# Full 128 by 128 tiles in the attentions of the second block

## The reference

```
proj = h @ w_in              # queries, keys, values, forget gates, branch gates
qa, ka = rms_norm(...)       # first attention: 8 heads of 64
log_f = log_sigmoid(fa + forget_bias);  c = cumsum(log_f)
# first attention, for head h, query i, key j <= i (16 learned tokens included)
s = qa.ka / 8 + c_i - c_j ;  p = softmax(s) ;  o_fox = p @ va
# second attention: 8 query heads of 64 over 2 key heads, a window of 128,
s = qb.kb / 8 + bias_by_distance ;  p = softmax(s with a sink) ;  o_swa = p @ vb
y = sigmoid(ga) * (o_fox @ w_branch_fox) + sigmoid(gb) * (o_swa @ w_branch_swa)
h = h + y @ w_out
```

## Time and profile before

| | |
|---|---|
| median of three runs | 2533.72 us |
| the profiled execution: time, span | 2534.61, 2532.8 us |
| TensorE busy | 2481.2 us, 98% |
| VectorE, ScalarE busy | 1899.5 us (75%), 1251.7 us (49%) |
| GpSimd busy | 125.7 us, 5% |
| DMA | 467.22 MB, 184 GB/s |

### The profile page before, as it was taken

One profiled execution on the slowest core, in us unless ns is written; L12 is line 12 of the kernel. 1 busy time (PEld: TensorE's weight loads), 2 busy tenths in 40 slices (PEclk: granted clock), 3 DMA queues, 4 the chain that ended last, 5 costly groups with the idle time before them and its releaser, 6 DMA issues.

```text
span 2532.8 us, 48392 instructions
## 1 busy us (share of the span) xinstructions
PE 2481.2 (98%) x17792; PEld 2279.1 (90%) x17792; DVE 1899.5 (75%) x3685; ACT 1251.7 (49%) x2079; POOL 125.7 (5%) x99
## 2 busy tenths in 40 slices
PE   9999999999999999999999999999999999999999
PEld 8999988999999889999989999998889998778999
DVE  6789997666666887889986666666877756667774
ACT  6754874444444434556864444444344445445443
POOL 0042000000000000061000000000000000000000
PEclk9999999999999999999999999999999999999999
DMA  7445677666655554445776666655545553534555
GB/s 241 142 153 177 194 203 237 210 207 208 215 194 188 185 188 167 167 160 190 199 236 214 208 211 207 211 185 188 189 152 175 171 187 124 110 126 136 181 179 163
DMA packets 192505, 467.22 MB, mean 184 GB/s; under 512 B 81747, under 2 KB 83795, under 8 KB 191457
## 3 DMA queue, kind: packets, MB, share of 16 engines
q1 hardware_dynamic: 118736, 419.99, 50.0%
q0 software_dynamic: 6992, 25.81, 3.7%
q10 hardware_dynamic: 66624, 19.40, 3.2%
HBM read 442.53 MB, written 22.61 MB: 184 GB/s over the span
## 4 chain that ended last, share of the span: by engine, by line
PE 48%; DVE 3%; DMA 1%; ACT 1%; issue 0%; DVEq 0%; ACTq 0%
PE acc L842 14%; PE work L522 9%; PE work L524 9%; PE work L523 9%; PE acc L522 1%; PE acc L523 1%; PE work L856 1%; PE acc L524 1%; DMA ring<-in_gate_in 1%; DVE ring_lo L516 1%; PE work L1071 1%; PE work L1043 0%; PE work L695 0%; DVE arena L2125 0%; PE work L697 0%
## 5 line engine op out<-in xcount | busy, mean ns | idle before, releaser
L516 DVE TENSOR_TENSOR ring_lo<-ring,ring_hi 128x1024 fp32r<-128x1024 f32 x758 | 920.2, 1217 | 431.3 <-ACT ring_hi L510 429.6
L510 ACT ACTIVATE ring_hi<-ring 128x1024 fp32r<-128x1024 f32 (+1 forms) x798 | 832.6, 1051 | 460.5 <-PE acc L842 369.9
L522 PE MATMUL work<-normed_hi,ring_hi 128*128 128x256 f32 (+1 forms) x2512 | 715.3, 285 | 21.3 <-DVE ring_lo L516 13.9
L523 PE MATMUL work<-normed_lo,ring_hi 128*128 128x256 f32 (+1 forms) x2512 | 709.4, 282 | 0.0
L524 PE MATMUL work<-normed_hi,ring_lo 128*128 128x256 f32 (+1 forms) x2512 | 707.1, 281 | 0.0
L842 PE MATMUL acc<-ring_hi,weighed 128*128 128x512 f32 x2048 | 588.3, 396 | 4.8 <-DVE weighed L1947 4.8
L522 PEld LDWEIGHTS work<-normed_hi,ring_hi 128*128 128x128 f32 x2512 | 473.5, 189 | 35.7 <-DVE ring_lo L516 13.7
L523 PEld LDWEIGHTS work<-normed_lo,ring_hi 128*128 128x128 f32 x2512 | 474.7, 189 | 7.9
L524 PEld LDWEIGHTS work<-normed_hi,ring_lo 128*128 128x128 f32 x2512 | 473.4, 188 | 0.0
L842 PEld LDWEIGHTS acc<-ring_hi,weighed 128*128 128x128 f32 x2048 | 373.7, 188 | 83.8 <-DVE weighed L1947 5.2
L522 PE MATMUL work<-arena_parts,ring_hi 128*128 128x256 f32 (+1 forms) x1184 | 337.5, 285 | 1.8 <-ACT arena L1151 1.1
(11 more groups left out here) (289 smaller groups left out, 2505.3 us busy)
## 6 DMA issues: line engine op xcount, KB each, us to landing
ring<-in_u SPq DMA_DIRECT2D x256, 512.0 KB, 3.3
ring<-in_v SPq DMA_DIRECT2D x256, 512.0 KB, 3.3
ring<-in_ffn_in SPq DMA_DIRECT2D x88, 512.0 KB, 3.3
ring<-in_query SPq DMA_DIRECT2D x32, 512.0 KB, 3.3
ficients_of_later_chunks<-gate_b ACTq DMA_DIRECT2D x32, 512.0 KB, 4.6
arena<-ficients_of_later_chunks POOLq DMA_DIRECT2D x32, 512.0 KB, 4.1
ring<-in_ffn_out SPq DMA_DIRECT2D x32, 512.0 KB, 3.9
ring<-in_even_in SPq DMA_DIRECT2D x27, 512.0 KB, 4.2
```

Source lines behind the costliest of these rows:

```text
L510: act.activation(ring_hi[:, n % RING, 0:width], ring[:, n % RING, 0:width], ACT.Copy).then_inc(hi_ready, 1)
L516: eng.tensor_tensor(ring_lo[:, n % RING, 0:width], ring[:, n % RING, 0:width], ring_hi[:, n % RING, 0:width].bitcast(F32), ALU.subtract).t ...
L522: pe.matmul(out, w_hi, hi, start=start, stop=False, **more)
L523: pe.matmul(out, w_hi, lo, start=False, stop=False, **more)
```

## The change

The transposes, value products and key bias are made of full 128 by 128 tiles. Rows of `scores2` grow from 276 to 384 columns, and the buffer moves onto rows of `forget` that are done with. The last block of values is cleared once, so that its rows behind the 16 are zero, and each of the two value heads of the second attention is stored twice side by side. The value product writes all 128 partitions, of which the half of the head is read. The high and low part of the cumulated gates stand in partitions 0 to 7 and 32 to 39 of one zeroed tile, and the signs likewise, so that the bias is one product over 128 partitions. The signs (`neg_head`) are read as 128 partitions in place of 8. GpSimd has two more clearings at the start of its part and, at the end of it, clears the columns behind each row of `scores2`; TensorE waits for these (`pads_ready`) ahead of its first two turns.

```diff
         val2 = view("mix", [6, 3, P])
+        scores2 = arena[:, forget_at + TA:forget_at + TA + 4 * 3 * P].rearrange("p (b t) -> p b t", b=4)
...
+            pool.memset(val2[:, :, 2, :], 0.0).then_inc(memset_done, 1)
+            pool.memset(forget_two[:, :].bitcast(F32), 0.0).then_inc(memset_done, 1)
...
-                             (neg_head[0:FOXH, :, :], a["neg_head"]),
+                             (neg_head[:, :, :], a["neg_head"]),
...
                     pool.dma_start(bias2[:, t, :, lo:lo + width], src).then_inc(bias_in, 16)
+            pool.wait_ge(*freed(W0["mix"] + MIX_ITEMS.index(("turnf", 0))))
+            pool.wait_ge(forget_lo, 1)
+            for t in range(NT):
+                n = META + P * (t + 1)
+                pool.memset(scores2[:, t::NT, n:P * (t + 2)], 0.0).then_inc(pads_ready, 1)
...
-                            for x in range(2):
-                                mm = pe.matmul(work[:, w % 4, 0:keys], neg_parts[0:FOXH, h, :], forget_two[0:FOXH, x, 0:keys], start=False, stop=(x == 1))
+                            mm = pe.matmul(work[:, w % 4, 0:keys], neg_parts[:, h, :], forget_two[:, 0:keys], start=False, stop=True)
...
                         pe.wait_ge(probs_ready, n_before + u + 1)
+                        if u < NT:
+                            pe.wait_ge(pads_ready, NT)
                         for b in range(t + 2):
-                            lo, hi = b * P, min((b + 1) * P, keys)
-                            mm = pe.transpose(work[0:hi - lo, w % 4, b * P:(b + 1) * P], scores2[:, u % 4, lo:hi], ident)
+                            mm = pe.transpose(work[:, w % 4, b * P:(b + 1) * P], scores2[:, u % 4, b * P:(b + 1) * P], ident)
...
-                            v = val2[0:rows, h // 2, b, (h % 2) * HD2:(h % 2 + 1) * HD2] if fox else \
-                                val2[0:rows, 4, b, (h // 4) * HD2:(h // 4 + 1) * HD2]
-                            mm = pe.matmul(work[half, w % 4, t * P:S], v, prob2[0:rows, u % 2, b, t:NT, :].rearrange("p t q -> p (t q)"),
+                            v = val2[:, h // 2 if fox else 4 + h // 4, b, :]
+                            mm = pe.matmul(work[:, w % 4, t * P:S], v, prob2[:, u % 2, b, t:NT, :].rearrange("p t q -> p (t q)"),
...
                     elif kind == "swaval":
                         act.wait_ge(*done(w))
-                        act.activation(val2[:, 4, 0:2, :], work[:, w % 4, 0:S].rearrange("p (t d) -> p t d", t=2), ACT.Copy)
-                        act.activation(val2[0:META, 4, 2, :], work[0:META, w % 4, S:S + P], ACT.Copy).then_inc(bank_free[w % 4], 1)
+                        for g in range(2):
...
+                            act.activation(twice(val2[:, 4 + g, 0:2, :]), main.unsqueeze(2).to_broadcast([P, 2, 2, HD2]), ACT.Copy)
+                            ins = act.activation(val2[0:META, 4 + g, 2, :].rearrange("p (x d) -> p x d", x=2), meta.unsqueeze(1).to_broadcast([META, 2, HD2]), ACT.Copy)
...
-                    act.activation(prob2[:, h % 2, 0:t + 1, t, :], work[:, w % 4, 0:(t + 1) * P].rearrange("p (b q) -> p b q", q=P), ACT.Copy)
-                    act.activation(prob2[0:META, h % 2, t + 1, t, :], work[0:META, w % 4, (t + 1) * P:(t + 2) * P], ACT.Copy).then_inc(bank_free[w % 4], 1)
+                    if t:
+                        empty(w, prob2[:, h % 2, :, t, :], work[:, w % 4, 0:3 * P].rearrange("p (b q) -> p b q", q=P))
+                    else:
...
```

More of the change, by code:

```diff
@@ L55 @@
 NB = 32
+HALF_ROW = 32
 EVEN_ITEMS = [
@@ L399, in build @@
         qk2raw = view("mix", [BEHIND, TA])
-        scores2_at = used["mix"]
         qk2sq = view("mix", [BEHIND, TA])
-        scores2 = arena[:, scores2_at:scores2_at + 4 * (TA + 4)].rearrange("p (b t) -> p b t", b=4)
         qk2ms = view("mix", [BEHIND, TA])
         bias2 = view("mix", [NT, FOXH, TA])
-        val2 = view("mix", [5, 3, P])
+        val2 = view("mix", [6, 3, P])
         prob2 = view("mix", [2, 3, 2, P])
@@ L421, in build @@
         w_forget = view("mix", [K, FOXH])
+        forget_two = view("mix", [TA], arena_parts)
         mix_y = view("after", [2, S])
@@ L1067, in attend @@
                         for b in range(NT + 1):
[L1068 to L1071 removed]
+                            t = max(b - 1, 0)
+                            v = val2[:, h // 2 if fox else 4 + h // 4, b, :]
+                            mm = pe.matmul(work[:, w % 4, t * P:S], v, prob2[:, u % 2, b, t:NT, :].rearrange("p t q -> p (t q)"),
                                            start=(b == 0), stop=(b == NT), skip_group_check=True)
@@ L1484, in mix @@
                     elif kind == "lastval":
+                        if j == 0:
+                            act.wait_ge(memset_done, 9)
                         empty(w, val2[0:META, 2 * j:2 * j + 2, 2, :], work[0:META, w % 4, 0:S].rearrange("p (h d) -> p h d", h=2))
@@ L1487, in mix @@
                         act.wait_ge(*done(w))
-                        act.activation(val2[:, 4, 0:2, :], work[:, w % 4, 0:S].rearrange("p (t d) -> p t d", t=2), ACT.Copy)
-                        act.activation(val2[0:META, 4, 2, :], work[0:META, w % 4, S:S + P], ACT.Copy).then_inc(bank_free[w % 4], 1)
+                        for g in range(2):
+                            twice = lambda v: v.rearrange("p t (x d) -> p t x d", x=2)
+                            cols2 = slice(g * HD2, (g + 1) * HD2)
+                            main = work[:, w % 4, 0:S].rearrange("p (t d) -> p t d", t=2)[:, :, cols2]
+                            act.activation(twice(val2[:, 4 + g, 0:2, :]), main.unsqueeze(2).to_broadcast([P, 2, 2, HD2]), ACT.Copy)
+                            meta = work[0:META, w % 4, S + g * HD2:S + (g + 1) * HD2]
+                            ins = act.activation(val2[0:META, 4 + g, 2, :].rearrange("p (x d) -> p x d", x=2), meta.unsqueeze(1).to_broadcast([META, 2, HD2]), ACT.Copy)
+                        ins.then_inc(bank_free[w % 4], 1)
                     elif kind == "turnf":
                         act.wait_ge(forget_ready, 1)
-                        act.activation(forget_two[0:FOXH, 0, :], forget[0:FOXH, 0, :], ACT.Copy).then_inc(forget_hi, 1)
+                        act.activation(forget_two[0:FOXH, :], forget[0:FOXH, 0, :], ACT.Copy).then_inc(forget_hi, 1)
                         empty(w, forget_col, work[:, w % 4, 0:NT * FOXH].rearrange("p (t h) -> p t h", t=NT))
@@ L1522, in turn_copy @@
                         act.wait_ge(*done(w0 + ATT_ITEMS.index(("mix", h - 2))))
-                    act.wait_ge(*done(w))
-                    act.activation(prob2[:, h % 2, 0:t + 1, t, :], work[:, w % 4, 0:(t + 1) * P].rearrange("p (b q) -> p b q", q=P), ACT.Copy)
-                    act.activation(prob2[0:META, h % 2, t + 1, t, :], work[0:META, w % 4, (t + 1) * P:(t + 2) * P], ACT.Copy).then_inc(bank_free[w % 4], 1)
+                    if t:
+                        empty(w, prob2[:, h % 2, :, t, :], work[:, w % 4, 0:3 * P].rearrange("p (b q) -> p b q", q=P))
+                    else:
+                        act.wait_ge(*done(w))
+                        act.activation(prob2[:, h % 2, 0, t, :], work[:, w % 4, 0:P], ACT.Copy)
+                        act.activation(prob2[0:META, h % 2, 1, t, :], work[0:META, w % 4, P:2 * P], ACT.Copy).then_inc(bank_free[w % 4], 1)
                 softmax(ATT_ITEMS, w0, "att", scores2, HEADS * NT, lambda u: META + P * (u % NT + 1) + (0 if u < FOXH * NT else 1), turn_copy, beside)
@@ L2212, in fixed_arrays @@
     late = {"foxmask": np.stack([np.where(cols[None, :] <= META + P * t + q, 0.0, NEG) for t in range(NT)], axis=1).astype(f)}
-    eye = np.eye(FOXH)
-    late["neg_head"] = np.repeat(-eye[:, :, None], P, axis=2).astype(f)
+    late["neg_head"] = np.zeros((P, FOXH, P), f)
+    for h in range(FOXH):
+        late["neg_head"][[h, HALF_ROW + h], h, :] = -1.0
     def bucket(d):
```

10 lines of the change are left out of this document (4 added, 6 removed).

## The result

The changed kernel takes 2561.17 us at the median (2560.24 to 2563.15) against 2533.72 (2532.06 to 2535.68) before: a ratio of 1.0109, 95% interval 1.0098 to 1.0119. It is slower by 27.5 us, where 25.8 were forecast. The profiled execution took 2562.32 us, with a span of 2560.4.

A forecast was written before the change was run, and what follows sets the result against it. TensorE, busy 98% of the span, was taken as the bound. 2534.6 + 32.9 + 0.3 + 2.5 - 9.7 = 2560.6; the runs' median lies 0.9 lower, 2559.7, rounded to 2559.5 us, with an 8-in-10 range of 2553 to 2567.

The forecast's parts named there:

- Turn 0 near 2222.6, +32.9 us: TensorE's first turn of the attention stage waits for GpSimd's last memsets, behind the bias write: 2222.6 against 2189.71.
- The write no quicker once the loads stop: GpSimd's bias write of 2.6 MB keeps its pace while TensorE stands and loads no more gates: 0 us taken.
- rival B: The bias write speeds up as gate loads stop: 3.6 us less, 2556; with all 16 engines, 2545. Chance 10%.
- The gain, 9.7 us behind turn 0: Saved shape switches on TensorE in both attentions: 0.99 us a head in the first, 0.41 in the second.
- rival C: Wider value-product weights cost what the switches save: 5.3 us of the gain lost, 2565, or 2569 without any. Chance 12%.
- 0.06 us at a turn: The first query block's turn, transposes on TensorE, was to shorten from 0.37 to 0.31 us; the other turn wins nothing.
- The clock, 2.5 us: After TensorE's 34 us stand, a 6.8 us stretch at half clock loses 0 to 3.4 us; 2.5 taken.
- The constants, 0.3 us: GpSimd's extra clearing and larger read of bias signs delay constants by 1.5 to 4.0 us, mostly covered; 0.3 taken.
- rival A: Pads behind the score rows are ready before turn 0, so nothing stands and only gains remain: 2522.8 us. Chance 5%.

The follow-up runs named there:

- the halves: The changed kernel with the bias write cut into two DMAs of 64 copies each, both waited for: 2562.03 us, ratio 1.0112.
- the kernel kept at full clock: The changed kernel with 150 matmuls of zeros on an unused bank ahead of TensorE's first turn, during its wait: 2559.18 us, ratio 1.0108.
- the kernel with early pads: The changed kernel with GpSimd's clearing of the columns behind the scores moved ahead of its wait for the bias write: 2527.57 us, ratio 0.9975.
- making the copies from memory: On top of the early clearing of score columns, the bias table's 8 rows are written to memory once and copied 128 times from there: 2524.74 us, ratio 0.9960.
- the one with 64 value columns: The kernel with bias copies made from memory, but value products with 64 columns of weights again, the last block keeping 128 rows: 2527.09 us, ratio 0.9973.

## Why the prediction was right

Step by step, by the changed kernel's profile:

- *Turn 0 near 2222.6, +32.9 us.* It starts at 2222.39, +32.68. The wait alone, added to the kernel before, brings it to 2222.05.
- *The write no quicker once the loads stop (rival B).* It took 55.62 us of waiting in place of 56.02. The forecast was right. Of its two supports the rows held (7 engines' worth in both windows), but a bound by the number of engines, from which rival B drew its 2545, is not what holds the write: with the halves the share went to 82.6% and the wait became longer. What the limit is stays open between the source and the form of the write.
- *The gain, 9.7 us behind turn 0.* A head gains 1.00 and 0.42 us where 0.99 and 0.41 were worked out, so rival C is out. Two of its terms, value product and key bias, were found again by distances (+3.6 and +4.1 us when undone, the last value block of 16 rows left out). The third, 0.06 us at a turn, exists but was booked to the turn; it belongs to the value product, and that its sum came out all the same is luck.
- *The clock, 2.5 us.* 2.6 by the kernel kept at full clock. Turn 0 to last score is then 9.2 less and 2.6 more, -6.6, as measured. The term was a choice between 0 and 3.4, so that it came out to 0.1 us is in part luck.
- *The constants, 0.3 us.* The first split of the stage starts at 2106.76 in place of 2106.58, and GpSimd's first memset is late by the same 0.18 us: nothing. The read of 512 KB landed in 4.4 us, as fast as the 32 KB, so both estimates of its price were too high.

The sum was 1.7 us low against the profiled execution. That is the low-clock stretch in the later stages (+1.9 from the last turn to the end), for which the prediction had no term; it comes and goes between profiles. What the prediction did not ask is what else lay under the wait. Without it the kernel with early pads came to 2527.57, 4.8 us above rival A's 2522.8; making the copies from memory gave back 2.8 of them, and where the other 2 lie is not shown.

## What to carry to other kernels

Ask of every new wait where the thing that is waited for stands in its engine's program, and what that engine waits for ahead of it: two memsets of 0.3 us held TensorE's first turn up by 33 us, because they stood behind an unrelated DMA. Where short products alternate with full ones, read the distances from start to start at each change of shape, since a switch can cost as much as the short product; but try each widening alone, for one of three brought nothing and carried the whole price. And when a wait is removed, look for the next one under it before you count the gain.

## What the runs showed of the hardware

- A write of 2624 KB from 8 partitions of the on-chip memory took 56.5 us with 44% of the 16 DMA engines' time and 57.4 us, in two halves, with 83%: some 47 GB/s either way. The same bytes from memory to memory, in packets four times as long, took 13.7 us.
- Transposes with 16 columns of weights behind ones with 128, and ahead of a score over 64 partitions, cost no more than full ones (0.31 us for the turn with either). A value product with 64 columns costs 0.3 us more than one with 128. A score over 64 partitions costs 0.8 us a head more than one over 128 (6.18 to 5.42, 5.95 to 5.17; two scores a head), and two bias products over 8 partitions 0.58 us a head more than one over 128 (two biases a head).
- Low-clock stretches of 3.4 or 6.8 us follow gaps of 1.5 to 3 us in some profiles and not in others with the same gaps. A gap of 2.5 us near 2158 has 6.8 us at 0.50 behind it in the kernel before and none in the one with 64 value columns. Profiles with a stretch of 3.4 us 33 us behind the last turn are 1.1 to 1.9 us longer from there to the end.
